# Forget gates as fp32 products in four column groups, bias copies split in eight, and weight splits ahead of row work

## The chip, the cores and the metric

The kernel runs on one core of one Trainium2 chip. Its time is the device time of one execution in microseconds (us); lower is better. The times given are the median of three runs with their lowest and highest; the profile is of one further execution.

## The reference, cut to what matters

One encoder layer is applied to two groups of tokens with shared weights: 528 prompt tokens (16 learned meta tokens and 512 frames) and 64 new frames of a running stream whose last 128 keys and values are cached. Everything is fp32.

```python
z = h @ w_in                       # 2048 -> heads' q, k, v, gates g, and 16 forget columns ff
lf = log_sigmoid(ff + b_f)         # one value per token and forgetting head
c = cumsum(lf)                     # over the tokens (prompt; cached 128 and then the 64 new)
# 16 forgetting heads ("Fox"):
s = q @ k.T * SCALE + c[query] - c[key];  s = where(key <= query, s, -1e30);  o = softmax(s) @ v
# 16 sliding-window heads in 4 key/value groups ("Swa"), T5 bias from rel_bias by distance, and a sink:
s = q @ k.T * SCALE + bias;  p = exp(s - m) / (sum(exp(s - m)) + exp(sink - m));  o = p @ v
mix = concat(o_fox * silu(g_fox), o_swa * silu(g_swa)) @ w_out
y = layer_norm(ALPHA * h + mix)
```

The outputs are y for both groups, the new keys and values of all heads, and `lf` itself.

## The kernel before, in words

**Tiling.** Activations lie transposed: 16 chunks (`ko`) of 128 features by 592 tokens (`TOK`), in two halves of 296 tokens (`HALF`). The projection weights come as 52 tiles of 128 output columns by 2048 features, those of the output as 16 more. To have nearly fp32 results from the fast fp32r product, each operand is split in a high part (a copy in fp32r, made by ScalarE, ACT) and a low part (raw minus high, made by VectorE, DVE), and a product is three matmuls: high by high, high by low, low by high. Two weight tiles make a "duo"; its halves of the features are combined as in Strassen's scheme, which gives 15 units of 12 matmuls for TensorE (PE) in a duo, and needs sums of weight blocks (`make_seven`, `make_five`, `make_six`, `make_four` on DVE), each of them split in high and low again (`seven_part`, `back_parts` and the like, on ACT and then on DVE).

**Stretches.** `whole` writes the same plan for each engine. A stretch is one or two duos; in it the projections of the next pair of heads stand on PE together with the attention of the pair before. The first stretch has one duo (`first=True`, 15 steps) and no attention; then come 8 stretches of two duos with Fox attention, 7 with Swa attention (one of two duos, six of one), and a final one that runs beside the output projection. Step `s` of a stretch holds unit `u` of its duo `k`. In each step every engine goes through a fixed list in order (`run` of each engine): what comes later in the list waits for all before it. Every engine works its queue in order.

**One tile of attention.** There are five query tiles to a pair. Tile i has its scores at step `score_at[i]` (PE `score`, DVE `scores`: bias, mask, maximum), exponentials a step later (ACT `probabilities`), reciprocals two steps later (DVE `reciprocals`, ACT `scale_rows`), transposes at `score_at[i] + 4` (PE `turn`), copied by ACT (`keep_turned`), and values (PE `values`).

**In a step of ACT before the change:** `keep_turned`, `probabilities`, `scale_rows`, then the weight parts of this step (`inside`), then the rest. **In a step of DVE:** `reciprocals`, the joins of a unit's result (`join`), `scores`, then `split(st, *ready)` (the low part of q or k, or the SiLU; each waits for ACT to evacuate first), `keep_values`, the low part of the cached keys, and only then the weight parts. The back half of the second tile of a duo (`back_parts(d, 1)`) is at u == 4 on ACT and at u == 6 on DVE; unit 8 is the first to need it.

**The opening.** `opening_products` on PE runs while x and the first two weight tiles (v, g) come in, in 9 parts of x (`X_CUTS`). Ahead of each part's products it makes the forget columns: weights `wff_parts` hold high, high again and low (48 columns), and each of them meets x high and x low in both halves: four matmuls of 296 columns to a chunk, into partitions 0 to 47 of `ps[:, O_BANK + h]`. The parts at 0, 16 and 32 are summed afterwards. The parts of `wff` are made by two ACT copies and a DVE subtraction before anything else.

**The gates before:** at step 1 (`LOGS_AT`) ACT copies partitions 32 to 47 of both banks to `e` (`gates`), DVE adds the bias and takes |z|, ACT takes exp(-|z|), DVE makes 1 + e, and a reciprocal of 16 rows by 592; ACT takes the logarithm. At step 4 (`SUMS_AT`) DVE finishes lf (written over the first rows of `kT`) and makes three running sums (`cT`). At step 1 and 2 stand also `last_sums`, the splits of the third sum of x blocks and of a changed x block, which unit 6 needs. `turn_gates` on PE at step 7 turns `cT`; `bias_table` on DVE at step 9 writes the rows of the Swa bias (31 small copies).

**GpSimd (POOL)** fills constants and issues DMAs, in order. Before the first stretch it waits for `bias_made` (the table), stores it, clears `q2`, waits for `c_ready`, stores `cT` and lf, clears `k_low`, `pt_meta`, `v_nat`; only then does it load the running sums (`cbc`), the cached keys (`kc`) and values. PE's unit at step 12 of the first stretch needs `zeros`, DVE's join of k needs `lf_stored`, since lf lies in `kT`. In the first Swa stretch POOL makes one DMA of all 16 rows of the bias to 128 copies each (`rel_copies`, DRAM to DRAM), waits for it, and loads the bias of each pair from it.

**SyncE (SP)** issues the weight loads, 512 KB each, each when the DVE's low part of the data before is made: `right_low`, `four_made`, `back_low[1]`, `back_low[0]`, in this order in each duo.

```python
                    for i in st.at(st.score_at, s - 2):      # ACT, ahead of the weight parts
                        scale_rows(st, i)
```

Of the kernel before, what the change touches and what calls it, by code (L numbers as in the profile page):

```python
# [24 lines left out]
F32 = mybir.dt.float32  # L25
# [5 lines left out]
P = 128  # L31
# [3 lines left out]
N_HEADS = 16  # L35
# [34 lines left out]
LOGS_AT, SUMS_AT, GATES_TURNED_AT, TABLE_AT, V_FIRST_AT = 1, 4, 7, 9, 12  # L70
LAST_SUMS_AT = 1
# [217 lines left out]
def build(nc, xT, w_all, w_ff, b_f, lf_cache, k_cache, v_cache, sinks, rel, keep_k, keep_v,  # L289
          x_p, x_s, ln_g, ln_b, y_p, y_s, fkT, fvT, lf_out, skT, svT, kept_k, kept_v):  # L290
    ctx = ExitStack()
    with ctx:
# [66 lines left out]
        bf = sb("bf", [N_HEADS, 1], F32)  # L359
# [6 lines left out]
        wff_parts = sb("wff_parts", [P, KO, 3, N_HEADS], F32R, at=cbc_at + TOK * 4)  # L366
# [4 lines left out]
        gate_terms = sb("gate_terms", [N_HEADS, 5, TOK], F32, at=keys_at)  # L371
        z, e, u1, wk, az = (gate_terms[:, i, :] for i in range(5))
# [42 lines left out]
        wff_high, wff_low = sem("wff_high"), sem("wff_low")  # L415
# [5 lines left out]
        x_high, x_low = sem("x_high"), sem("x_low")  # L421
        sum_made, sum_high, sum_low = sem("sum_made"), sem("sum_high"), sem("sum_low")
# [142 lines left out]
        def _(sp):  # L565
            sp.dma_start(wff, w_ff).then_inc(wff_loaded, 16)
            for what, i in opening:
# [5 lines left out]
                if what == "x" and i == 1:  # L573
                    for dst, src in ((bf[:], b_f), (lfc, lf_cache), (relT, rel),
                                     (sink[:], sinks.partition_broadcast(P))):
                        sp.dma_start(dst, src).then_inc(small_loaded, 16)
# [80 lines left out]
        def _(pool):  # L657
# [23 lines left out]
            pool.wait_ge(sum_made, 4)  # L681
            nc.gpsimd.memset(q2[:, 2 * NQ:].bitcast(F32), 0.0).then_inc(zeros, 1)
            pool.wait_ge(c_ready, 3)
            pool.dma_start(c_rows, cT[:]).then_inc(c_stored, 16)
            pool.dma_start(lf_out, lfT).then_inc(lf_stored, 16)
            pool.wait_ge(zeros, 2)
            nc.gpsimd.memset(k_low[HD:P, 0, :].bitcast(F32), 0.0).then_inc(zeros, 1)
            pool.wait_ge(zeros, 3)
            nc.gpsimd.memset(k_low[0:HD, 1, :].bitcast(F32), 0.0).then_inc(zeros, 1)
            pool.wait_ge(sum_low, 4)  # L690
            nc.gpsimd.memset(pt_meta[:], 0.0).then_inc(zeros, 1)
            pool.wait_ge(c_stored, 16)
            pool.wait_ge(cq_turned, 1)
            nc.gpsimd.memset(v_nat[:, Values.META, :], 0.0).then_inc(zeros, 1)
# [1335 lines left out]
```

## Time and profile before

| | |
|---|---|
| median of 3 runs | 1079.94 us (1077.12 to 1082.41) |
| the profiled execution | 1080.62 us, its span 1078.8 us |
| PE / DVE / ACT / POOL busy | 95% / 67% / 50% / 5% of the span |
| mean granted TensorE clock | 0.983 |
| DMA | 109 GB/s over the span |

The span is the time from the first to the last instruction. An engine's busy share counts the time in which at least one of its instructions ran. PE's idle time is what can be won or lost without changing its work; the granted clock says how fast it ran in a stretch.

### The profile page before, as it was taken

To read this page: it belongs to the slowest core of one execution; us is meant where nothing else is said; L and a number is where in the kernel's file an instruction comes from. 1 tells how busy PE (TensorE), PEld (TensorE's weight loads), DVE (VectorE), ACT (ScalarE), POOL (GpSimd) and SP (SyncE) were. 2 spreads that over 40 slices of the span, in tenths; PEclk is the share of its full clock that TensorE was granted. 3 is DMA by queue.
4 is the path that set the end of the run, shared out by engine and by line. 5 is a ranking of instruction groups with operands and counts; after the bars stand their busy time and mean duration, and the time that the engine had idled before them with its cause. 6 is when DMAs were issued, how large, how long until landed. Compare 5 with 4: busy or idle time off the path is not lost.

```text
span 1078.8 us, 20251 instructions
## 1 busy us (share of the span) xinstructions
PE 1025.7 (95%) x7287; PEld 951.8 (88%) x7287; DVE 721.0 (67%) x1454; ACT 534.2 (50%) x1219; POOL 58.8 (5%) x117
## 2 busy tenths in 40 slices
PE   8957999999999999999979999999999999999996
PEld 7957999999999999999979889899899878888884
DVE  6686768685867768685856877676776764332486
ACT  6425646464654646465544766564766672111310
POOL 1011000101000000100001000010000000000000
PEclk9978999999999999999989999999999999999998
DMA  9012322323232222323432322132322653222413
GB/s 334 32 64 89 106 92 77 128 89 116 86 110 72 92 99 89 132 89 99 154 113 76 109 88 72 52 104 69 109 89 94 240 194 101 79 78 94 179 60 117
DMA packets 31297, 115.00 MB, mean 107 GB/s; under 512 B 4352, under 2 KB 4768, under 8 KB 28624
## 3 DMA queue, kind: packets, MB, share of 16 engines
q1 hardware_dynamic: 24320, 87.26, 23.3%
q0 software_dynamic: 6928, 27.08, 7.4%
q8 instruction: 31, 0.51, 0.2%
q14 instruction: 18, 0.15, 0.0%
HBM read 99.31 MB, written 18.29 MB: 109 GB/s over the span
## 4 chain that ended last, share of the span: by engine, by line
PE 54%; DVE 20%; ACT 10%; issue 10%; DMA 4%; DVEq 1%; POOL 0%; SPq 0%; ACTq 0%; POOLq 0%
PE ps L1856 19%; PE ps L1618 16%; PE ps L1628 10%; DVE wl L1089 5%; PE ps L1822 4%; DMA w_raw<-in_w_all 3%; PE ps L1796 2%; ACT tb L901 2%; DVE tb L1266 2%; ACT k L879 1%; ACT q L874 1%; DVE small L1287 1%; DVE tb L1272 1%; ACT wh L815 1%; DVE small L1285 1%
## 5 line engine op out<-in xcount | busy, mean ns | idle before, releaser
L1618 PE MATMUL ps<-xh,wh 128*128 128x296 f32 (+1 forms) x864 | 264.2, 306 | 10.1 <-DVE wl L1089 9.7
L1618 PE MATMUL ps<-xh,wl 128*128 128x296 f32 (+1 forms) x864 | 257.6, 298 | 0.0
L1618 PE MATMUL ps<-xl,wh 128*128 128x296 f32 (+1 forms) x864 | 257.4, 298 | 0.0
L1856 PE MATMUL ps<-wh,mix_parts 128*128 128x512 f32 x576 | 186.2, 392 | 0.0
L1618 PEld LDWEIGHTS ps<-xh,wh 128*128 128x128 f32 x864 | 164.1, 190 | 17.2 <-DVE wl L1089 15.2
L1618 PEld LDWEIGHTS ps<-xl,wh 128*128 128x128 f32 x864 | 164.3, 190 | 0.0
L1618 PEld LDWEIGHTS ps<-xh,wl 128*128 128x128 f32 x864 | 163.9, 190 | 0.0
L1089 DVE TENSOR_TENSOR wl<-w_raw,wh 128x1024 fp32r<-128x1024 f32 (+1 forms) x150 | 142.9, 953 | 22.7 <-ACT wh L815 12.6
L1628 PE MATMUL ps<-xh,wh 128*128 128x296 f32 x400 | 123.4, 309 | 13.7 <-DVE mid_part L1164 7.3
L1856 PEld LDWEIGHTS ps<-wh,mix_parts 128*128 128x128 f32 x576 | 108.1, 188 | 24.2 <-issue 0.7
L901 ACT ACTIVATE tb<-tb,small 128x256 f32<-128x256 f32 (+5 forms) x160 | 81.3, 508 | 94.6 <-DVE small L1285 71.0
L1856 PE MATMUL ps<-wl,mix_parts 128*128 128x512 f32 x320 | 125.0, 391 | 0.0
L1628 PE MATMUL ps<-xl,wh 128*128 128x296 f32 x400 | 120.5, 301 | 0.0
L1628 PE MATMUL ps<-xh,wl 128*128 128x296 f32 x400 | 120.2, 301 | 0.0
L913 ACT ACTIVATE tb<-tb,small 128x256 f32<-128x256 f32 (+4 forms) x160 | 72.1, 498 | 40.8 <-DVE small L1300 40.1
L1628 PE MATMUL ps<-sum_high,wh 128*128 128x296 f32 x300 | 92.1, 307 | 0.0
L1628 PEld LDWEIGHTS ps<-xh,wh 128*128 128x128 f32 x400 | 76.4, 191 | 15.3 <-DVE xl L1089 7.5
L1628 PE MATMUL ps<-sum_low,wh 128*128 128x296 f32 x300 | 89.7, 299 | 0.0
L1628 PE MATMUL ps<-sum_high,wl 128*128 128x296 f32 x300 | 89.7, 299 | 0.0
L1085 DVE TENSOR_TENSOR wl<-w_raw,wh 128x1024 fp32r<-128x1024 f32 x32 | 38.1, 1222 | 69.0 <-ACT wh L803 68.9
L1628 PEld LDWEIGHTS ps<-xl,wh 128*128 128x128 f32 x400 | 76.6, 192 | 0.0
L1628 PEld LDWEIGHTS ps<-xh,wl 128*128 128x128 f32 x400 | 76.3, 191 | 0.0
(195 smaller groups left out, 1740.5 us busy)
## 6 DMA issues: line engine op xcount, KB each, us to landing
w_raw<-in_w_all SPq DMA_DIRECT2D x106, 512.0 KB, 3.9
w_raw<-in_w_all SPq DMA_DIRECT2D x14, 1024.0 KB, 4.8
cbc<-c_rows POOLq DMA_DIRECT2D x16, 360.0 KB, 4.2
x_raw<-in_xT SPq DMA_DIRECT2D x7, 592.0 KB, 10.1
rows<-in_x_p POOLq DMA_DIRECT2D x4, 1024.0 KB, 5.2
out_y_p<-rows SPq DMA_DIRECT2D x16, 256.0 KB, 2.5
mix_rows<-mixT POOLq DMA_DIRECT2D x14, 288.0 KB, 2.4
rel_copies<-rel_rows POOLq DMA_DIRECT2D x1, 3072.0 KB, 18.6
```

The source lines that it names most:

```text
L815: nc.scalar.activation(wh[f][:, BACK], w_raw[f][:, BACK], ACT.Copy).then_inc(back_high[f], 1)
L874: nc.scalar.activation(q2[r, at:at + width], home(f, h)[r, result(tile, h)], ACT.Copy, scale=SCALE).then_inc(q_high, 1)
L901: nc.scalar.activation(t, t, ACT.Exp, bias=nm, accum_out=total[:, i % 3, head:head + 1]).then_inc(exp_done, 1)
L913: nc.scalar.activation(row, row, ACT.Copy, scale=recip[:, i % 3, head:head + 1]).then_inc(scaled, 1)
L1085: nc.vector.tensor_tensor(wl[slot][:, a], w_raw[slot % 2][:, a], wh[slot][:, a].bitcast(F32), ALU.subtract).then_inc(w_low, 1)
L1089: nc.vector.tensor_tensor(low, raw, high.bitcast(F32), ALU.subtract).then_inc(done, 1)
L1266: ins = nc.vector.scalar_tensor_tensor(out=rows_[:, head, a:b], in0=st.score_out(ps, head, piece, b - a), scalar=cqp[:, i, head:head + 1], ...
L1618: ins = nc.tensor.matmul(ps[:, bank, result(tile, h)], a[f][:, w], b[:, ko, first:first + width], start=(ko == n_first and i == 0), stop=( ...
L1628: ins = nc.tensor.matmul(ps[:, bank, 0:HALF], a[:, w], b[:, j, :], start=(start and j == 0 and i == 0), stop=(stop and j == CUT - 1 and i ...
L1796: ins = nc.tensor.transpose(st.turn_out(ps, head, j), tb[:, i % SLOTS, head, first:first + P], ident[:])
L1822: ins = nc.tensor.matmul(ps[head_rows(head), bank, at:at + q], v_nat[:, block_, HD * head:HD * head + HD], moving[:, head, 0:q], start=(j ...
L1856: ins = nc.tensor.matmul(ps[:, bank, :], a, b[slot][:, w], start=(ko == 0 and i == 0), stop=(ko == KO - 1 and i == len(products) - 1))
```

## The change

In the opening, the forget columns are now plain fp32 products straight from `x_raw` and `wff`, without splits: for each chunk and half one product of 16 columns, even and odd chunks apart, each of the four in its own group of 32 columns of the array (`tile_position`), so that results lie at partitions 0, 32, 64 and 96. They wait for the DMA of x alone and stand ahead of PE's wait for `x_low`. The gate arithmetic works on one tensor of 80 partitions by 296 (half 0 at partition 0, half 1 at 64), and its steps are spread: inputs and 1 + e in `opening_splits`, reciprocals at step 3, logarithm and lf at step 5, running sums at step 7; `turn_gates` moves from step 7 to 9, `bias_table` from 9 to 13, v's turn from 12 to 13. `last_sums` goes into `opening_splits`. lf lies in `tb` and no longer in `kT`.

POOL's opening is in another order: cached keys first, then v's store, cT, the clears, the running sums, cached values, and the bias table and k's store last. The copies of the bias are made two heads at a time, one DMA at the start of each stretch that has Fox attention; the first Swa stretch waits for all eight.

In all stretches: ACT's `scale_rows` stands behind the weight parts of its step; DVE's `split`, `keep_values` and the low part of the cached keys too; `back_parts(d, 1)` moves to u == 3 on ACT and u == 5 on DVE.

```diff
-LOGS_AT, SUMS_AT, GATES_TURNED_AT, TABLE_AT, V_FIRST_AT = 1, 4, 7, 9, 12
-LAST_SUMS_AT = 1
+GATES_TURNED_AT, TABLE_AT, V_FIRST_AT = 9, 13, 13
+GATE_ROWS = 80
+BIAS_COPIES = FOX_PAIRS
...
-        gate_terms = sb("gate_terms", [N_HEADS, 5, TOK], F32, at=keys_at)
+        gate_terms = sb("gate_terms", [P, 5, HALF], F32, at=keys_at)
...
-        lfT = kT[0:16, :]
+        lfT = tb[0:16, 0, :, :].rearrange("p a b -> p (a b)")[:, 0:TOK]
...
# POOL
-            pool.wait_ge(bias_made, 1)
-            pool.dma_start(rel_rows, bias_rows).then_inc(bias_stored, 16)
-            ...
+            def first_loads(st):
+                pool.wait_ge(gates_summed, 1)
+                pool.wait_ge(x_low, X_PARTS)
+                nc.gpsimd.memset(gate_terms[0:GATE_ROWS, 0:2, :], 0.0).then_inc(z_cleared, 1)
+                pool.wait_ge(sum_made, 4)
+                nc.gpsimd.memset(q2[:, 2 * NQ:].bitcast(F32), 0.0).then_inc(zeros, 1)
+                pool.wait_ge(sum_low, 4)
+                nc.gpsimd.memset(pt_meta[:], 0.0).then_inc(zeros, 1)
+                pool.dma_start(kc[:], k_cache[0]).then_inc(k_cached, 16)
+                pool.wait_ge(v_read, 1)
+                pool.wait_ge(v_first, 1)
+                pool.dma_start(fvT[0:P, :], vT[:]).then_inc(v_stored, 16)
+                pool.wait_ge(c_ready, 3)
+                pool.dma_start(c_rows, cT[:]).then_inc(c_stored, 16)
...              # k_low cleared, lf stored, running sums loaded, v_nat cleared, cached values loaded
+                pool.wait_ge(bias_made, 1)
+                pool.dma_start(rel_rows, bias_rows).then_inc(bias_stored, 16)
...
+            def copy_bias(i):
+                two = bass.ds(2 * i, 2)
+                pool.dma_start(rel_copies[two], rel_rows[two, :].rearrange("h (o n) -> h o n", o=1)
+                               .broadcast_to([2, P, REL])).then_inc(bias_copied, 16)
...
-                if st.own is Swa and st.kind is Fox:
-                    pool.dma_start(rel_copies, ...16 heads...).then_inc(bias_copied, 16)
-                    pool.wait_ge(bias_copied, 16)
+                if st.kind is Fox:
+                    copy_bias(st.g)
...
# ACT, opening_splits
-                act.wait_ge(wff_loaded, 16)
-                nc.scalar.activation(wff_parts[:, :, 0, :], wff, ACT.Copy).then_inc(wff_high, 1)
-                nc.scalar.activation(wff_parts[:, :, 1, :], wff, ACT.Copy).then_inc(wff_high, 1)
...
                 front_parts(1, (passed, 1))
+                act.wait_ge(sum_made, 3)
+                nc.scalar.activation(sum3_high[:], raw3[:], ACT.Copy).then_inc(sum_high, 1)
+                act.wait_ge(z_cleared, 1)
+                act.wait_ge(gates_summed, 1)
+                for h in range(2):
+                    ins = nc.scalar.activation(gate_half(e, h), ps[HD * h + 32:HD * h + 32 + N_HEADS, O_BANK + h, 0:HALF],
+                                               ACT.Copy)
+                ins.then_inc(gates_joined, 1)
                 seven_part(1, (passed, 2))
                 six_part(1, (passed, 2))
+                act.wait_ge(sum_made, 4)
+                nc.scalar.activation(xh[:, first_x, late], x_raw[:, first_x, late], ACT.Copy).then_inc(sum_high, 1)
                 ...            # v's evacuation
                 back_parts(1, 0, (projected[1], 1))
+                act.wait_ge(gate_step, 2)
+                nc.scalar.activation(e, az, ACT.Exp, scale=-1.0).then_inc(gate_exp, 1)
                 ...            # the two Tanh
                 act.wait_ge(gate_step, 3)
                 nc.scalar.activation(az, u1, ACT.Ln).then_inc(gate_exp, 1)
...
# ACT, each step
-                    for i in st.at(st.score_at, s - 2):
-                        scale_rows(st, i)
...
-                        if u == 4:
+                        if u == 3:
                             back_parts(d, 1, (projected[1], 2) if st.first else (unit_done, st.after(k, -1)))
...
+                    for i in st.at(st.score_at, s - 2):
+                        scale_rows(st, i)
                     if st.kv is not None and s == st.cached_at:
                         cached_high(st)
...
# DVE, opening_splits
                 nc.vector.tensor_tensor(x21, x21, x22, ALU.subtract).then_inc(sum_made, 1)
+                gate_inputs()
+                dve.wait_ge(sum_high, 3)
+                low_of(sum3_low[:], raw3[:], sum3_high[:], sum_low)
+                gate_ones()
                 back_parts(1, 0)
-                dve.wait_ge(sum_made, 4)
                 for h in range(2):
                     silu(st, h, (first_part, diff_part)[h], ps[:, 2 + h, :])
+                dve.wait_ge(sum_made, 4)
+                dve.wait_ge(sum_high, 4)
+                low_of(xl[:, first_x, late], x_raw[:, first_x, late], xh[:, first_x, late], sum_low)
...
# DVE, each step
-                    if ready is not None:
-                        split(st, *ready)
-                    ...         # keep_values, low part of the cached keys
                     if inside:
...
+                        if u == 5:
+                            back_parts(d, 1)
                         if u == 6:
                             four_part(d)
-                            back_parts(d, 1)
...
+                    if ready is not None:
+                        split(st, *ready)
+                    ...         # keep_values, low part of the cached keys
                     if st.first:
-                        if s == LOGS_AT:
-                            ...
+                        if s == 3:
+                            gate_reciprocals()
+                        if s == 5:
                             gate_logs()
-                        if s == SUMS_AT:
+                        if s == 7:
                             gate_sums()
...
# PE, opening_products
+                def gate_products(two):
+                    for h in range(2):
+                        for odd in range(2):
+                            ko, to = 2 * two + odd, HD * h + 32 * odd
+                            ins = nc.tensor.matmul(ps[to:to + N_HEADS, O_BANK + h, 0:HALF], wff[:, ko, :],
+                                                   x_raw[:, ko, h * HALF:(h + 1) * HALF],
+                                                   start=(two == 0), stop=(two == KO // 2 - 1), tile_position=(0, to))
+                    return ins
...
-                    pe.wait_ge(x_low, i + 1 if i < X_PARTS - 3 else X_PARTS)
-                    for ko in ahead(i):
-                        ...
+                    for two in ahead(i):
+                        if two == ahead(i)[0] or i == X_PARTS - 3:
+                            pe.wait_ge(x_loaded[...the part that holds chunk 2 * two + 1...], 16)
+                        ins = gate_products(two)
                     if i == X_PARTS - 3:
                         ins.then_inc(gates_summed, 1)
+                    pe.wait_ge(x_low, i + 1 if i < X_PARTS - 3 else X_PARTS)
```

Waits that go with the moved data: DVE's join of the first k no longer waits for `lf_stored`, its first split of k waits for `zeros` 5 (was 4), its first score waits for `lf_stored`; ACT's first `keep_turned` waits for `bias_stored`; PE's first turn of v waits for `cq_ready` 2 as well.

## Rows read from the trace of the kernel before

**Rows 1.** The page, its part 1: busy time, share, instructions.
```profile
PE 1025.7 (95%) x7287; PEld 951.8 (88%) x7287; DVE 721.0 (67%) x1454; ACT 534.2 (50%) x1219; POOL 58.8 (5%) x117
```

**Rows 2.** Waits of PE, whole span: who waited for whom, us in total, times, longest.
```profile
PE ps L1618 <- DVE wl L1089: 9.7, 11, 3.2
PE ps L1628 <- DVE mid_part L1164: 7.3, 1, 7.3
PE ps L1628 <- DVE mid_part L1197: 6.4, 1, 6.4
PE ps L1822 <- ACT pt_meta L923: 4.9, 1, 4.9
PE ps L1796 <- ACT pt_meta L923: 4.5, 6, 0.9
...
PE ps L1796 <- ACT pt L921: 2.4, 5, 0.5
```

**Rows 3.** Windows: length; busy us of PE, PEld, DVE, ACT, POOL; PEclk; DMA share, GB/s.
```profile
59.60:66.30 6.70, 3.64 (x15) 3.67 (x16) 6.60 (x9) 0.63 (x1) 0.00 (x0) 0.50 0.27 97
...
69.90:76.50 6.60, 4.83 (x19) 4.83 (x20) 6.46 (x29) 0.46 (x1) 0.00 (x0) 0.50 0.23 79
...
90.30:97.00 6.70, 3.17 (x13) 3.17 (x14) 5.45 (x12) 2.58 (x4) 0.00 (x0) 0.50 0.01 2
...
547.80:554.40 6.60, 3.71 (x27) 3.32 (x28) 4.62 (x8) 4.25 (x9) 0.00 (x0) 0.50 0.04 14
```

**Rows 4.** Timeline of DVE, 38 to 82: start us, duration us, what, [idle before].
```profile
38.48 1.38 DVE L1374 TENSOR_TENSOR x_raw<-x_raw 128x1184 f32<-128x1184 f32 x1
...
51.33 0.95 DVE L1394 SCALAR_TENSOR_TENSOR gate_terms<-ps,bf,gate_terms 16x296 f32<-16x296 f32 x2 [4.66 <-ACT gate_terms L973]
...
54.82 3.84 DVE L1406 RECIPROCAL gate_terms<-gate_terms 16x592 f32<-16x592 f32 x1
...
66.07 1.25 DVE L1428 TENSOR_TENSOR_SCAN cT<-cbc,kT 16x528 f32<-16x528 f32 x1
...
75.14 2.27 DVE L1333 COPY pt<-pt 16x165 f32<-16x165 f32 x31
81.04 0.47 DVE L1197 TENSOR_TENSOR kT<-ps,diff_part 128x296 f32<-128x296 f32 x1 [3.63 <-DMA out_lf_out<-kT]
```

**Rows 5.** Timeline of ACT, 88 to 90.
```profile
88.36 1.26 ACT L892 ACTIVATE k<-kc 64x128 fp32r<-64x128 f32 x4 [4.94 <-DMA kc<-in_k_cache]
```

**Rows 6.** Timeline of PE: first matmul of unit 3, second duo.
```profile
101.28 0.30 PE L1628 MATMUL ps<-xh,wh 128*128 128x296 f32 x1
```

**Rows 7.** Timeline of PE: fp32 and fp32r products.
```profile
6.92 0.30 PE L1726 MATMUL ps<-xl,wff_parts 128*48 128x296 f32 x1
...
115.19 0.29 PE L1618 MATMUL ps<-xh,wl 128*128 128x280 f32 x1
115.42 1.09 PE L1822 MATMUL ps<-pt,v_nat 128*64 128x128 f32 x16
116.34 0.39 PE L1822 MATMUL ps<-pt_meta,v_nat 128*64 128x128 f32 x4
```

**Rows 8.** Timeline of ACT, DVE and PE in a Fox stretch, steps 4 to 8.
```profile
229.15 1.04 ACT L815 ACTIVATE wh<-w_raw 128x1024 fp32r<-128x1024 f32 x1
...
233.29 1.22 DVE L1089 TENSOR_TENSOR wl<-w_raw,wh 128x1024 fp32r<-128x1024 f32 x1
...
234.56 0.40 PE L1618 MATMUL ps<-xh,wh 128*128 128x280 f32 x1 [0.68 <-DVE wl L1089]
```

**Rows 9.** Timeline of DVE and ACT in a Swa stretch, steps 6 and 7.
```profile
642.27 0.45 DVE L1205 SCALAR_TENSOR_TENSOR mixT<-last_part,first_part 128x280 f32 x1 [1.69 <-ACT last_part L867]
...
644.77 0.91 ACT L913 ACTIVATE tb<-tb,small 128x256 f32<-128x256 f32 x2 [2.81 <-DVE small L1300]
```

**Rows 10.** The page's part 6, and ACT's timeline at 548.
```profile
rel_copies<-rel_rows POOLq DMA_DIRECT2D x1, 3072.0 KB, 18.6
...
548.52 1.06 ACT L809 ACTIVATE wh<-w_raw 128x1024 fp32r<-128x1024 f32 x1 [7.04 <-DMA w_raw<-in_w_all]
```

More of the change, by code:

```diff
@@ L715, in run @@
             def run(st):
+                if st.first:
+                    first_loads(st)
+                    return
                 g, kv = st.pair, st.kv
-                before = st.kind is not None
-                if st.own is Swa and st.kind is Fox:
-                    pool.dma_start(rel_copies, rel_rows.rearrange("h (o n) -> h o n", o=1)
-                                   .broadcast_to([N_HEADS, P, REL])).then_inc(bias_copied, 16)
-                    pool.wait_ge(bias_copied, 16)
+                if st.kind is Fox:
+                    copy_bias(st.g)
                 if st.turn_before is not None and not st.final:
@@ L737, in run @@
                 if st.own is Fox:
-                    pool.wait_ge(c_stored, 16)
-                    if before:
-                        pool.wait_ge(score_read, Fox.base(g))
+                    pool.wait_ge(score_read, Fox.base(g))
                     pool.sem_inc(pool_passed, 1)
@@ L766, in run @@
                                    ).then_inc(v_cached, 16)
-                    if before and not st.keep:
+                    if not st.keep:
                         store_mixed(st.g)
@@ L1189, in join @@
                 if h == 0 and tile == "k":
-                    if st.first:
-                        dve.wait_ge(lf_stored, 16)
-                    else:
+                    if not st.first:
                         dve.wait_ge(k_stored, 16 * st.kv)
@@ L1494, in run @@
                             five_part(d)
-                        if st.first and s == LAST_SUMS_AT + 1:
-                            last_sums()
                         if u == 4:
@@ L1698, in ahead @@
                 def ahead(i):
-                    if i > X_PARTS - 3:
+                    if i == 0 or i > X_PARTS - 3:
                         return ()
-                    return range(x_part(i).start, KO if i == X_PARTS - 3 else x_part(i).stop)
+                    return range(x_part(i).start // 2, KO // 2 if i == X_PARTS - 3 else x_part(i).stop // 2)
+                def gate_products(two):
+                    for h in range(2):
+                        for odd in range(2):
[4 more added lines that the diff above has]
+                    return ins
                 def some(k, h, chunks):
@@ L1832, in turn_values @@
                     pe.wait_ge(zeros, 7)
+                    pe.wait_ge(cq_ready, 2)
                 else:
```

134 lines of the change are left out of this document (55 added, 79 removed).

## The prediction

> **What bounds the kernel now.** The page's first part comes first: PE is busy for 95% of the span [rows 1], all others far less, so its work is the floor, and what is to be won lies in its idle time and its clock. Next the waits of PE over the whole span [rows 2]. Three groups are seen. In the first duo stand 7.3 us (before unit 6), 3.2 (before unit 8; the longest of the first row) and, before unit 0 of the second, 6.4. A single wait of 4.9 us stands before values at 550 us. The rest are small ones that come back in nearly each stretch: 6.5 us of L1618 on the back half of the second weight tile (9.7 minus 3.2), and 4.5 plus 2.4 us of transposes on ACT. Then the granted clock [rows 3]: after each long wait PE runs at 0.50, that is 1.2 GHz where 2.4 is the upper level. Of these windows PE works 3.64, 4.83, 3.17 and 3.71 us, and half of each is lost to the clock: 7.7 us in all, 5.8 of it in the first duo.
>
> DVE's timeline tells what the first duo waits for [rows 4]. From 51.33 DVE makes the gates in one piece, a reciprocal of 3.84 us among them, and the results that PE waits for stand behind. Later its join of k waits until lf has gone out by DMA (81.04), a DMA that POOL issues only after the table (75.14 and 2.27). ACT then waits 4.94 us for cached keys whose load stands behind the same POOL queue [rows 5]. So the first duo is bound by gates, table and POOL's order, not by PE.
>
> **The change, part by part.** The sums go against the profiled execution: 1080.62 us, span 1078.8, so 1.8 us lie around the span; the median of the runs shown is 0.7 lower.
>
> *Gates on PE.* Removed are 64 fp32r products of 296 columns (one of them in [rows 7]), one column per pulse of 2.4 GHz, 0.135 us from start to start with a little overhead. Added are 32 fp32 products of 296 columns. For their price: the values of one tile are ten fp32 products of 128 columns in two column groups and stand as 16 plus 4 records, two to a product; they take from 115.42 to 116.5 until the last one starts, about 0.107 us for each product, so 0.21 us for two side by side. At 296 columns one product is then 0.49 us. If four groups run side by side, 8 fours take 4.0 us; if only two do, 7.9; if none, 15.8. I take 4.0, since the row with groups shows full overlap, for two. Of it 0.5 us falls into times when PE waits for x anyway, while 60 of the old products (8.1 us) stood where PE is busy: a gain of about 4.5 us; 1.2 with two side by side, minus 5.7 with none.
>
> The Trainium skill ("TensorEngine Tiling (Array Packing)", Key Properties) says that a change of tiling mode drains the engine. The trace agrees in kind: 0.23 us pass from the last product before the block to its first, against 0.135 elsewhere [rows 7]. By that rule six insertions would cost about 1.2 us more, which lies in the bounds above.
>
> *The chain of DVE and ACT in the opening.* It decides, not the gates on PE, so I walk it with durations of rows. DVE's changed block of x ends at 38.48 + 1.38 = 39.86, as before (all ahead of it waits for DMA or is unchanged). Then inputs 0.95 and |z| 0.49 (half the columns), low part of the third sum 1.38, two small steps 0.55, back part 1.22 [rows 8], two SiLU 0.92, with some 0.9 of waiting for ACT's exp: 46.4. ACT may keep the first result 0.45 later, so unit 3 starts at about 46.9. ACT's block of x delays v's evacuation to 41.7, where PE, 4.5 us earlier, waits at most 0.5.
>
> DVE goes on: low part of the block 1.38, difference 0.46, five 0.68, middle 0.46, reciprocal 1.95 (half of 3.84): 51.1. Two weight parts 1.36, back part 1.22, four steps of logs 1.9: 55.6. Join, four, q's low parts, the two sums of five: 2.7. Running sums 1.25 and about 0.65: 60.2. PE, now without waits, has done unit 9 at 58.3 and waits 1.9 us to turn the gates. Then front, two sums, join, six: 3.7; k's low parts wait for ACT: 65.1; the cached keys, on whose load nobody waits now, 67.0; gates kept 67.35. PE comes to turn v at 65.5 and waits 1.8 us for that. At step 13 the table of 2.27 us and v's copies lie on DVE, so the last join of the duo ends at 75.75, where PE wanted its bank at 74.6: 1.2 us. The key's low parts and scores follow, and unit 3 of the second duo begins at 78.7. Before it began at 101.28 [rows 6]. The gain is 22.6 us; clock and waits that the rows of before show there are all in it. It is a walk of some forty steps without gaps, so I take 21, with ends of 12 and 26: 12 where two of the new waits let the clock fall and the chain slips by some 7 us, 26 where PE meets none of the new waits. The lower price of PE's gates changes this by little: 3 us more on PE are taken out of the two waits behind.
>
> *The bias copies.* Removed is the DMA of 3072 KB that took 18.6 us [rows 10]; the weight loads issued into it came so late that ACT waited 7.04 us, and PE 4.9. Eight copies of 384 KB at the start of stretches are 2.3 us each by that row. They lie beside a moment at which the loads under way are for a back half needed far later, so I cost them at nothing; without that cover each could hold ACT by up to 2.3 us, of which PE would see perhaps half, 9 us in all. Gain: 4.9 plus 1.9 of clock = 6.8, ends minus 2 and 6.8. POOL issues one DMA more per stretch, 0.5 us, ahead of v's store; whoever waits for that store has many steps.
>
> *Second tile's back half.* DVE ends it at 234.51 and PE's unit 8 starts at 234.56 after a wait of 0.68 [rows 8]. It stands at step 6 behind a join, scores of 2.6 us and another part. At step 5 it would end about 3.5 us earlier, since ACT has its high part made at step 3, in idle time, and no longer at 229.15. Gain 6.5 us [rows 2]; the end below is 0. What is late next: the scores of step 6 start 1.2 us later, and the exponentials and the transposes behind them; they have two steps (3.3 us) in hand.
>
> *Row scales and splits behind the weight parts.* In the Swa stretch DVE stands 1.69 us for a tanh and ACT 2.81 us for a reciprocal [rows 9], with weight parts queued behind both. These parts now fill such waits; the reciprocal comes 1.5 us earlier, ACT's copies too, by about 2 us. PE's waits there are 0.5 to 0.9 us [rows 2], so they go: 6.9 us, ends minus 5 and 6.9. What is queued behind the moved instructions: ACT's copies of the transposes, up to 1.9 us later where no wait is filled (step 13), for which PE has a step in hand. I take 6.0.
>
> *Sum.* 21 + 6.8 + 6.5 + 6.0 = 40.3. 1080.6 - 40.3 = 1040.3 for the execution, 0.7 lower for the median: I say 1040.
>
> **The rivals.**
>
> A: *the first duo gives half.* The gate chain is now on the path at steps 9 and 13. If POOL's longer chain (three clears, two loads of running sums, then v's places) or the cached keys hold PE for another 3 us at two places, and the clock falls after each, 10 us of the gain are gone: 1050. For it speaks that POOL's issues took 0.5 us each and that three such waits cut the clock before [rows 3]; against it, that POOL's part ends by 64.9 in my walk. 10%.
>
> B: *the repeated waits only move.* In every stretch the transposes wait for ACT, which now has the scales behind parts that themselves wait for PE's units. Then 12.5 us are not won: 1053. For: the scores at step 6 are later. Against: both engines have idle times of over 1 us in rows 9. 10%.
>
> C: *it is slower.* Place: ACT at steps 2, 5 and 11, where a part waits for a unit's end and the scales now wait behind it. PE's transposes need them two steps later. If that margin is gone, PE, ACT and DVE run in a lock step, and each such tile costs PE two parts of 0.6 us: 3.5 tiles of a stretch by 1.2 by 15 stretches are 63 us, 1103. It decides from 2.7 us lost per stretch on. Against it: the unit that the parts wait for is done a step before. 4%.
>
> D: *four column groups don't overlap.* The Trainium skill ("TensorE: Matmul & The Clock Gate", What overlaps and what doesn't) has matmuls start strictly in order; by that, two records on one group would let only neighbours overlap. As a mechanism of this kernel: at 15.8 us for the 32 products PE's opening ends some 10 us later than in my walk, of which 3.7 are taken out of the waits behind: 1047. With two side by side it stays at 1041. 6%.
>
> **How the numbers follow.** My forecast has 70%, 1034 to 1048 by itself; A, B and D 26% together, 1047 to 1053; C 4%. The range that leaves out about 2 in 10 goes from 1032 to 1055: the low end where the first duo gives 26 and all else its upper end, the high end past B. Faster by over 0.5% (5.4 us, about what a measurement of this kernel can tell from no change): all but C, and a rest for what I haven't seen: 0.93. Within: 0.02. Slower: 0.05.
>
> **What would show it.** Unit 3 of the second duo near 79 us, no wait of PE over 3 us before it, and waits on the turn of gates and of v of 1 to 3 us. The fp32 gate products in fours, four starting together every 0.25 us. No wait at 540 to 550, rel_copies eight times at 3 to 5 us. No wait of L1618 on DVE of 0.68 in the Fox stretches, and none of L1796 in the Swa ones. It is wrong if PE's waits after 110 us sum to over 10 us, or if its busy time rises by more than 5 us.

## The result and the profile after

| | before | after |
|---|---|---|
| median of four runs | 1080.25 us (1077.12 to 1082.41) | 1030.16 us (1030.02 to 1030.48) |
| span of the profiled execution | 1078.8 us | 1028.6 us |
| mean granted TensorE clock | 0.983 | 0.997 |

The kernel became faster by 4.6%: the ratio is 0.9539, with a 95% interval of 0.9515 to 0.9563. The median lies 9.8 us under the forecast of 1040 and 1.8 us under the low end of the range. The sign and the places of the gain were right, and its size was not: 50.2 us of span where the sum had 40.3. One execution of experiment 8's kernel took 3469.64 us, for which no row gives a reason; it is left out below.

The page of the kernel after, its parts 1, 2 and 4 (they answer to [rows 1]; the chain's PE share was 54% before):

```profile
PE 1006.8 (98%) x7287; PEld 936.7 (91%) x7287; DVE 718.2 (70%) x1454; ACT 532.7 (52%) x1217; POOL 66.7 (6%) x125
...
PEclk9999999999999999999999999999999999999998
...
PE 90%; DVE 4%; DMA 2%; issue 1%; ACT 1%; SPq 1%; DVEq 0%; ACTq 0%
```

Waits of PE, whole span, after; columns as in [rows 2]:

```profile
PE ps L1627 <- DVE wl L1357: 1.8, 1, 1.8
PE ps L1734 <- DVE vT L1344: 1.6, 1, 1.6
PE ps L1859 <- DVE cq L1446: 1.6, 1, 1.6
PE ps L1627 <- DVE xl L1349: 1.5, 1, 1.5
PE ps L1839 <- ACT pt_meta L941: 1.2, 2, 0.9
PE ps L1765 <- DVE cT L1438: 1.2, 1, 1.2
PE ps L1637 <- ACT vT L977: 1.1, 1, 1.1
PE ps L1637 <- DVE kT L1200: 0.8, 1, 0.8
...
```

Read them against [rows 2]. The repeated rows (10 of the 11 waits of L1618, 6 and 5 of L1796) are gone, and so are the three of over 3 us and the one at 550. Eight kinds are left, seven of them single ones in the first duo; the longest is 1.8 us, and after none does the clock fall. The windows that answer to [rows 3], with the same columns, are 20 to 60 us, the end of the first duo, and the stretch around 514.39, where the product starts that waited at 550 before:

```profile
20.00:60.00 40.00, 37.72 (x296) 34.72 (x294) 37.82 (x48) 21.77 (x30) 2.24 (x6) 1.00 0.38 144
60.00:78.00 18.00, 15.59 (x116) 15.12 (x115) 14.72 (x59) 9.13 (x20) 6.35 (x12) 1.00 0.30 84
509.50:521.50 12.00, 12.00 (x104) 11.66 (x103) 9.51 (x21) 8.65 (x20) 0.00 (x0) 1.00 0.16 59
```

DVE's timeline after, in the first duo (it answers to [rows 4]): the reciprocal, a running sum, cached keys, gates kept, the table, the join.

```profile
48.78 1.99 DVE L1411 RECIPROCAL gate_terms<-gate_terms 80x296 f32<-80x296 f32 x1
...
57.68 1.24 DVE L1438 TENSOR_TENSOR_SCAN cT<-cbc,tb 16x528 f32<-16x528 f32 x1
...
65.73 0.59 DVE L1236 TENSOR_TENSOR k_low<-kc,k 64x128 fp32r<-64x128 f32 x2 [1.69 <-ACT k L908]
...
66.49 0.15 DVE L1446 COPY cq<-ps 64x16 f32<-64x16 f32 x1
...
71.09 2.27 DVE L1338 COPY pt<-pt 16x165 f32<-16x165 f32 x31
...
74.43 0.45 DVE L1200 TENSOR_TENSOR kT<-ps,last_part 128x296 f32<-128x296 f32 x1
```

ACT's and PE's timelines after: the cached keys, which waited 4.94 us in [rows 5]; unit 3 of the second duo, at 101.28 in [rows 6]; a block of four gate products between two others.

```profile
64.43 1.27 ACT L908 ACTIVATE k<-kc 64x128 fp32r<-64x128 f32 x4
...
77.67 0.30 PE L1637 MATMUL ps<-xh,wh 128*128 128x296 f32 x1
```

```profile
9.04 0.29 PE L1627 MATMUL ps<-xh,wl 128*128 128x296 f32 x1
9.26 0.69 PE L1718 MATMUL ps<-x_raw,pt 128*16 128x296 f32 x8
9.89 0.41 PE L1627 MATMUL ps<-xh,wh 128*128 128x296 f32 x1
```

The block is four fp32 products (two records each) and takes 9.89 - 9.26 = 0.63 us with the change back to whole-array products.

The Fox stretch of [rows 8] and the Swa stretch of [rows 9], after:

```profile
197.45 1.04 ACT L831 ACTIVATE wh<-w_raw 128x1024 fp32r<-128x1024 f32 x1
...
203.83 1.22 DVE L1094 TENSOR_TENSOR wl<-w_raw,wh 128x1024 fp32r<-128x1024 f32 x1
...
208.45 0.30 PE L1637 MATMUL ps<-sum_high,wl 128*128 128x296 f32 x1
208.59 0.29 PE L1627 MATMUL ps<-xh,wh 128*128 128x280 f32 x1
...
601.11 0.45 DVE L1208 SCALAR_TENSOR_TENSOR mixT<-last_part,first_part 128x280 f32 x1 [0.19 <-issue]
...
602.55 0.89 ACT L929 ACTIVATE tb<-tb,small 128x256 f32<-128x256 f32 x2
```

DVE now ends its low part at 205.05, 3.5 us ahead of unit 8; it ended 0.05 us ahead before. DVE's wait of 1.69 is 0.19, and ACT's of 2.81 is gone.

The bias copies (page, part 6, answering to [rows 10]), and the one place where a copy is seen to hurt:

```profile
rel_copies<-rel_rows POOLq DMA_DIRECT2D x8, 384.0 KB, 10.7
...
391.77 1.06 ACT L825 ACTIVATE wh<-w_raw 128x1024 fp32r<-128x1024 f32 x1 [1.73 <-DMA w_raw<-in_w_all]
...
393.94 0.77 PE L1839 MATMUL ps<-pt,v_nat 128*64 128x128 f32 x10 [0.94 <-ACT pt_meta L941]
```

**Where the 50.2 us came from.** From unit 3 of the second duo on, PE issues the same 6786 matmuls in the same order in both kernels, so they can be laid side by side, start against start. Up to that unit 101.28 - 77.67 = 23.6 us are gained, behind it 26.5 more. Of these the stall at 550, with the slow clock behind it, is 6.8. The other 19.7 are the repeated waits, net of 1.0 given back at 393.94 and 0.6 in the first Fox stretch. The idle time shown on the 21 waits that went was 6.5 plus 6.9, so 13.4 us (13.5 unrounded).

Why more comes back than is shown can be read in three rows of PE's timeline before, around the wait of [rows 8] (its own row, 234.56, stands there):

```profile
233.45 0.29 PE L1628 MATMUL ps<-sum_low,wh 128*128 128x296 f32 x1
233.58 0.30 PE L1628 MATMUL ps<-sum_high,wl 128*128 128x296 f32 x1
...
234.79 0.29 PE L1618 MATMUL ps<-xl,wh 128*128 128x280 f32 x1
```

One product starts 0.13 us after the other (233.45, 233.58), yet each record is 0.30 long: it ends 0.16 us past the time at which the next would have started. Idle time is counted from that end. The wait shows 0.68, but from start to start 0.98 us pass where after the change 0.14 do (208.45 to 208.59): 0.84. The second product then starts 0.23 after the first instead of 0.13. So 0.95 us were lost where 0.68 are shown. In the alignment eight of the ten repeated waits of L1618 cost this 0.27 us more than they show, ten of the eleven of L1796 0.21 more, and three waits 0.07 more or nothing: 17.8 us for the 21, 4.3 more than shown. At eleven more places (nine of L1618, two of L1796) a product started 0.23 to 0.34 us late, with 0.07 us or less shown as idle: 3.2 us. 13.5 + 4.3 + 3.2 - 1.0 - 0.6 = 19.4; the last 0.3 is spread over small steps.

The Trainium skill ("Perfetto Trace Analysis", Tensor Engine Instruction) says that TensorE's end times are estimated, not observed. The rows agree: ends lie 0.16 us past the next start.

### The profile page after: what moved, and what is told of

Read it like the earlier page. It is cut to its first block, busy times and chain, and to the rows that moved or that the text cites. A ratio compares the mean times of both kernels' runs of the same rounds, so it can differ in the third digit from the quotient of the medians.

```text
span 1028.6 us, 20283 instructions
## 1 busy us (share of the span) xinstructions
PE 1006.8 (98%) x7287; PEld 936.7 (91%) x7287; DVE 718.2 (70%) x1454; ACT 532.7 (52%) x1217; POOL 66.7 (6%) x125
## 3 DMA queue, kind: packets, MB, share of 16 engines
q0 software_dynamic: 11856, 27.14, 8.0%
## 4 chain that ended last, share of the span: by engine, by line
PE 90%; DVE 4%; DMA 2%; issue 1%; ACT 1%; SPq 1%; DVEq 0%; ACTq 0%
PE ps L1627 30%; PE ps L1637 27%; PE ps L1874 20%; PE ps L1839 5%; PE ps L1813 4%; PE ps L1797 2%; PE ps L1796 2%; DMA x_raw<-in_xT 1%; DMA w_raw<-in_w_all 1%; DVE wl L1094 1%; PE ps L1859 1%; SPq L572 0%; PE ps L1817 0%; DVE tb L1271 0%; SPq L575 0%
## 5 line engine op out<-in xcount | busy, mean ns | idle before, releaser
L1627 PE MATMUL ps<-xh,wh 128*128 128x296 f32 (+1 forms) x864 | 261.3, 302 | 3.2 <-DVE wl L1357 1.8
L1627 PEld LDWEIGHTS ps<-xh,wh 128*128 128x128 f32 x864 | 162.5, 188 | 9.2 <-issue 6.2
L1627 PEld LDWEIGHTS ps<-xl,wh 128*128 128x128 f32 x864 | 162.8, 188 | 0.0
L1627 PEld LDWEIGHTS ps<-xh,wl 128*128 128x128 f32 x864 | 162.2, 188 | 0.0
L1637 PEld LDWEIGHTS ps<-xh,wh 128*128 128x128 f32 x400 | 75.2, 188 | 2.5 <-ACT vT L977 1.3
L1637 PEld LDWEIGHTS ps<-xl,wh 128*128 128x128 f32 x400 | 75.5, 189 | 0.0
L1637 PEld LDWEIGHTS ps<-xh,wl 128*128 128x128 f32 x400 | 75.1, 188 | 0.0
## 6 DMA issues: line engine op xcount, KB each, us to landing
rel_copies<-rel_rows POOLq DMA_DIRECT2D x8, 384.0 KB, 10.7
```

Of the source, the lines that this page charges most:

```text
L1627: ins = nc.tensor.matmul(ps[:, bank, result(tile, h)], a[f][:, w], b[:, ko, first:first + width], start=(ko == n_first and i == 0), stop=( ...
L1637: ins = nc.tensor.matmul(ps[:, bank, 0:HALF], a[:, w], b[:, j, :], start=(start and j == 0 and i == 0), stop=(stop and j == CUT - 1 and i ...
```

## Experiments

Four kernels start from the one before and make one part of the change alone, or three of its four; the others start from the kernel after. Each ratio is against runs of the kernel before taken beside that experiment (medians 1079.0 to 1079.8 us). Gains "from 101.28 on" are from the alignment described above, one trace each: ahead of that unit the traces with the old opening differ among themselves (it starts at 99.5 to 102.4 us).

**1. The back half of the second tile alone.**

```diff
-                        if u == 4:      # ACT; on DVE 6 becomes 5
+                        if u == 3:
                             back_parts(d, 1, ...)
```

> The kernel before with one edit: the back half of the second tile is split at u == 3 (ACT) and u == 5 (DVE). Theory S (a wait of PE costs what passes from start to start, which is about 0.16 us more than the idle time shown, because a matmul's record ends 0.16 us past the next one's start, and the second matmul after a wait starts 0.1 us late as well): all waits of L1618 on DVE go, and with them the small ones of 0.07 us that the table of waits leaves out: 11 us less, ratio 0.990. Theory I (a wait costs the idle time shown): 6.5 us less, ratio 0.994. If a new wait takes their place: under 3 us.

1065.85 us (1063.22 to 1066.94), ratio 0.9869 [0.9849, 0.9888]. From 101.28 on, 14.3 us are gained, against a sum of 6.5: 15.5 in the repeated waits, less 1.2 at the stall of 550, which got longer. Of PE's repeated waits these are left; all of L1618 are gone:

```profile
PE ps L1797 <- ACT pt L921: 2.4, 5, 0.5
PE ps L1797 <- ACT pt_meta L923: 1.7, 2, 0.9
```

A Fox stretch gives 1.28 us (0.95 + 0.33), which the start-to-start cost explains; the Fox stretches give 9.5 us in all, the Swa stretches 6.0. Of these 6.0, 2.0 are waits of L1618, and 3.8 are waits of L1796 (four of the eleven went), which the prediction had put down to the row work alone.

**2. The row work behind the weight parts alone.**

```diff
# ACT: scale_rows(st, i) from ahead of inside(...) to behind it
# DVE: split, keep_values and the cached keys' low part from ahead of the weight parts to behind them
```

> The kernel before with one edit: scale_rows on ACT and the splits, keep_values and the low part of the cached keys on DVE stand behind the weight parts of their step. Theory S: the waits of the transposes in the Swa stretches go (4.5 + 2.4 us shown, eleven of them): 8.7 us less, ratio 0.992. Theory I: 6.9 us less. The rival that the moved work makes transposes late elsewhere: less than 3 us, and new waits of L1796 in the Fox stretches. In the first duo, where the gates are still in one piece, either way within 1 us.

1059.12 us (1057.12 to 1060.85), ratio 0.9814 [0.9794, 0.9835]. From 101.28 on, 20.9 us: 3.4 at the stall of 550 (it shows 3.3 now), 17.5 in the repeated waits, against a sum of 6.0. The waits of L1796 are gone. Those of L1618 are shorter, about 0.25 us each (the longest of this row, 1.1, is in the first duo):

```profile
PE ps L1618 <- DVE wl L1089: 3.1, 9, 1.1
```

In the alignment that is 5.4 us in the Fox stretches and 12.1 in the Swa ones. Both theories had this far too low, since both gave each edit only one kind of wait. The measurement says that the two edits overlap: the back half alone takes all of what is lost in the Fox stretches and half of it in the Swa ones, the row work alone all in the Swa stretches and more than half (5.4 of 9.5) in the Fox ones.

**3. The bias copies alone.**

```diff
-                if st.own is Swa and st.kind is Fox:
-                    pool.dma_start(rel_copies, ...16 heads...)
+                if st.kind is Fox:
+                    copy_bias(st.g)
```

POOL's wait for the copies moves to the first stretch that loads a bias.

> The kernel before with one edit: eight bias copies of two heads at the start of the Fox stretches in place of one. The wait of 4.9 us of PE at 550 and the fallen clock behind it go: both theories 6.9 us less, ratio 0.9936. Should the copies delay weight loads, as one seems to in the changed kernel (ACT waits for a load at 390), 1 us of it is given back once or more.

1074.81 us (1073.71 to 1076.11), ratio 0.9953 [0.9937, 0.997]. 5.6 us from 101.28 on: the 6.8 of the stall, less 1.1 where ACT waits 3.18 us for a weight load beside a copy (issued at 409.24), and PE for ACT at 425.03:

```profile
PE ps L1826 <- ACT pt_meta L927: 1.1, 1, 1.1
```

In this trace unit 3 of the second duo started 1.1 us later than before, at 102.38, so the spans differ by 4.6 only. Being 0.5% of the time, this part is as small as such a comparison can tell.

**4. All three together, without the opening.**

> The kernel before with all three edits, so that only the opening and the gates are as before. Theory S: 26.5 us less, ratio 0.9755, and its first duo like that of the kernel before (unit 3 of the second duo near 101). Theory I: 19 to 20 us less, ratio 0.982; the rest of what the whole change gained would then have come from the first duo.

1051.36 us (1049.79 to 1053.89), ratio 0.974 [0.9718, 0.9761]. 27.6 us from 101.28 on, where the three alone add up to 40.8. They aren't additive: without the stall of 550 it is 20.9 us in the repeated waits, against 15.5 + 17.5 for experiments 1 and 2, which in part take the same waits away. The first duo still has its long waits:

```profile
PE ps L1633 <- DVE mid_part L1168: 7.3, 1, 7.3
PE ps L1846 <- POOL v_nat L695: 5.3, 1, 5.3
PE ps L1633 <- DVE mid_part L1201: 4.3, 1, 4.3
```

Its span is 1050.4, that of the kernel after 1028.6: gates and opening are worth 21.8 us (22.9 before unit 3 of the second duo, 1.1 given back behind it).

**5. Seven of eight gate products left out** (only the last block of four is made, so that the forget columns are of two chunks of the input alone).

> The changed kernel with only the last four of the 32 fp32 gate products (the forget columns are then of two chunks of the input alone; all else is the same). PE's opening is 7 blocks of 0.63 to 0.9 us shorter. Theory C (the chain of DVE and ACT sets the end of the first duo): v's evacuation and the gates' steps come no earlier, unit 3 of the second duo stays at 77.7 within 0.5, total 1030 within 0.7. Theory P (PE's products are on the path): 4 us less, 1026.

1031.06 us (1030.22 to 1031.82), ratio 0.9553 [0.953, 0.9577]: nothing won. What PE saves comes back as one longer wait, 4.9 us where it was 1.1, and around its end 6.8 us at the lower clock (39.6 to 46.5, granted 0.50). Unit 3 of the second duo starts at 78.73, 1.1 us later than in the kernel after and outside the 0.5 that was expected: 0.5 of it is there when the long wait ends (42.47 against 42.01), the rest comes behind it, where the clock is low at first.

```profile
PE ps L1637 <- ACT vT L977: 4.9, 1, 4.9
```

**6. Four gate products in two column groups** (odd chunks in the columns of the even ones, in other banks, from which ACT then copies them; the results are the same).

```diff
-                            ko, to = 2 * two + odd, HD * h + 32 * odd
+                            ko, to, bank = 2 * two + odd, HD * h, ((O_BANK + h, (T_BANK, SIDE)[h])[odd])
```

> The changed kernel with the odd chunks' gate products in the same two column groups as the even ones, in other banks: at most two products side by side. If four groups do run side by side, a block of four products takes about 0.5 us more than the 0.63 of the changed kernel (1.0 to 1.2 from its first start to the next product). In total, theory C: 0 to 0.5 us more, since PE has 3.7 us of waits behind it; theory P: 4 us more.

1030.73 us (1030.11 to 1032.15), ratio 0.9553 [0.9528, 0.9577], not told apart from four groups. PE's timeline, the same block:

```profile
9.16 1.18 PE L1718 MATMUL ps<-x_raw,pt 128*16 128x296 f32 x8
10.28 0.40 PE L1627 MATMUL ps<-xh,wh 128*128 128x296 f32 x1
```

10.28 - 9.16 = 1.12 us against 0.63: a second pair adds 0.49, the price that the prediction had for one product. So four groups do work side by side, and 8 blocks save 3.9 us of PE, nearly all of it hidden. What the new gates bring is then DVE's, ACT's and POOL's: their work was cut, spread and put in another order, and PE's was not the bound. Which of the three brings how much of the 22.9 us no run here takes apart.

**7. The copy of the bias in one piece, but early** (one DMA of 3072 KB at the start of the second stretch).

> The changed kernel with one bias copy of 3072 KB at the start of the second stretch in place of eight of 384 KB. Theory L (a copy this long holds up any weight load issued into its 18 us): loads issued at 83 to 85 land late by 8 to 10 us, PE stands 4 to 6 us and its clock falls: 6 to 7 us more, 1037. Rival M (only the moment in the first Swa stretch was bad): no change, 1030.

1036.6 us (1036.16 to 1037.78), ratio 0.9603 [0.958, 0.9626]. It lies from 76.42 to 95.30 us; three weight loads issued at 83.35 to 85.86 land at 93.79 to 97.63. The wait, and a window behind it (length, busy us of the five engines, clock, DMA):

```profile
PE ps L1840 <- ACT pt_meta L942: 6.7, 1, 6.7
...
95.40:102.00 6.60, 3.42 (x25) 3.10 (x26) 4.33 (x7) 4.25 (x9) 0.00 (x0) 0.52 0.02 8
```

It costs 6.9 us behind unit 3 of the second duo, about what the stall at 550 cost. So the eight pieces help since each is short, not since they come early.

**8. The bias table in idle time of DVE** (after the second part of x), the gates turned at step 10 and kept at the head of step 11.

> The changed kernel with the bias table made on DVE in its idle time after the second part of x (9.3 to 11.6 us), the gates turned at step 10 and kept at the head of DVE's step 11. Theory C: three waits of PE go (gates 1.2, v's turn 1.6, the last join 0.8, each 0.16 more from start to start): 4.1 us less, 1026. Rival: POOL's clears and loads, which end at about 65, take the place of the second wait, and k's join of the third: 1 to 2 us less, 1028.5.

1028.85 us (1028.4 to 1029.77, three executions), ratio 0.9531 [0.9501, 0.956]: about 1 us, which the ratios don't tell from none. The waits on `cT` and `kT` went, but the one on `cq` grew:

```profile
PE ps L1860 <- DVE cq L1449: 2.8, 1, 2.8
```

The copy of the gates stood at the head of step 11, behind the cached keys' low part of step 10, which waits for ACT until 65.7. Its place in DVE's list was wrong (mended in 12).

**9. The back half late again, in the kernel after.**

> The changed kernel with one edit undone: the second tile's back half stands again one step later on ACT and DVE. Theory T (each of PE's repeated waits has two causes in DVE's and ACT's order, and either edit takes most of them away): in the kernels built on the one before, the step alone gave 14.3 us from 101.28 us on, the row work alone 20.9, the bias copies 5.6, and all three together 27.6; so without the step 27.6 - (20.9 + 3.5) = 3.2 us come back, about 1033.5, as small waits of L1627 in the Fox stretches. Rival S (the edits add up): 11 to 14 us come back, 1041 to 1044.

1034.15 us (1034.05 to 1034.44), ratio 0.9581 [0.9565, 0.9597]: 4.0 us come back, as small waits, all in the Fox stretches in the alignment. That is near the 3.2 of theory T, and far from the 11 to 14 of its rival. The row of PE's waits:

```profile
PE ps L1626 <- DVE wl L1094: 2.6, 8, 0.8
```

**10. The row work ahead again, in the kernel after.**

> The changed kernel with the other edit undone: scale_rows on ACT, and the splits, the kept values and the cached keys' low part on DVE, stand ahead of the weight parts again. Theory T: 27.6 - (14.3 + 5.6) = 7.7 us come back, about 1038, nearly all of it in the Swa stretches, as waits on pt (L1796); next to nothing in the Fox stretches. Rival S (the edits add up): 17 to 21 us, 1047 to 1051, in both kinds of stretches.

1040.56 us (1039.85 to 1041.05), ratio 0.9639 [0.9623, 0.9655]. 10.4 us come back; in the alignment 1.5 of them before unit 3 of the second duo, 2.5 in the Fox stretches and 6.0 in the Swa ones. Two rows of PE's waits and one of ACT's timeline:

```profile
PE ps L1839 <- ACT pt_meta L941: 3.2, 6, 1.5
PE ps L1813 <- ACT pt L939: 2.5, 5, 0.5
...
151.67 1.06 ACT L825 ACTIVATE wh<-w_raw 128x1024 fp32r<-128x1024 f32 x1 [0.73 <-DMA w_raw<-in_w_all]
```

The second row is in the Swa stretches, as expected. The first is in the Fox stretches, where the theory had expected next to nothing. The third shows ACT waiting for a weight load some 14 us after a bias copy was issued (137.83), and the same stands at 212.04 and 272.42; that ACT has less in hand for it with the row work ahead is argued, not shown. Experiments 9 and 10 bear out that the edits overlap: undone singly they give back 4.0 and 10.4, where alone they had gained 15.5 and 17.5 in the repeated waits. They also fit experiments 1 and 2 place by place: the 4.0 are what the row work alone had left in the Fox stretches (9.5 - 5.4), and the 6.0 are the half of the Swa waits that the back half alone had left.

**11. The bias copies with the 128 copies outermost.**

```diff
-                pool.dma_start(rel_copies[two], ....rearrange("h (o n) -> h o n", o=1).broadcast_to([2, P, REL]))
+                pool.dma_start(rel_copies[two].rearrange("h p n -> p h n"),
+                               ....rearrange("h (o n) -> o h n", o=1).broadcast_to([P, 2, REL]))
```

> The changed kernel with each of the eight bias copies walked in another order: the 128 copies are the outermost dimension and the two heads the inner one, same bytes. Theory E (the 10.7 us from issue to landing come from the outermost dimension of two, which leaves the 384 KB to few of the 16 DMA engines): landing falls to 3 to 4 us, the one copy that meets ACT's weights near 390 us no longer does, and the time is 0 to 1.5 us lower, 1029. Rival F (a cost of each copy whatever its shape, or of the DRAM it writes): it stays near 10.7 us, and so does the wait.

1029.47 us (1029.07 to 1030.64), ratio 0.954 [0.9524, 0.9556], not told apart in time. The page, parts 6 and 3, and the row of PE's waits in which the 0.94 of 393.94 stood:

```profile
rel_copies<-rel_rows POOLq DMA_DIRECT2D x8, 384.0 KB, 5.1
...
q0 software_dynamic: 7120, 27.08, 7.9%
...
PE ps L1840 <- ACT pt_meta L942: 0.2, 1, 0.2
```

That wait is gone; the 0.2 that the row still has is another, at the first values. Behind unit 3 of the second duo 1.4 us are gained in the alignment. Landing falls from 10.7 to 5.1 us, not quite to 3 to 4, and the queue's packets from 11856 to 7120 for the same bytes. The order of the dimensions is the cause of half of the time. The trace's packets show how: a copy's 84 data packets of 4608 bytes take 7.9 us with two heads outermost, and 2.0 of them are under way at a time on average; with the 128 copies outermost, 80 such packets take 2.9 us, 6.7 at a time (medians of the eight copies). Some 1.7 us pass before the first of them and 0.4 behind the last. The 588 packets of 12 bytes that each copy had, and that are gone, run for some 2 us beside the first data packets; these go on for 6 us more. The Trainium skill ("DMA: Bandwidth & Descriptors", Rules for kernel authors) says that an outermost dimension of c < 16 keeps a DMA on at most c engines. The trace agrees: two heads were outermost, and two packets were under way.

**12. All that the experiments point to:** the table in idle time, the gates turned and kept in step 10 ahead of the cached keys, and the copies of 11.

> The changed kernel with the waits left in its opening worked away: the bias table in DVE's idle time after the second part of x, the gates turned and kept at step 10 and kept ahead of the cached keys, and the bias copies with 128 outermost. Theory G: the waits of PE on cq 1.6, on cT 1.2 and on kT 0.8 us go, and the copy's 0.9, each worth 0.16 us more than it shows: about 4 to 5 us less than the changed kernel, 1026. Rival H: what stands next in the order (POOL's clears for cached values, ACT's copy of v) holds PE instead, and 2 us at most are won: 1028.

1026.06 us (1025.91 to 1026.17), ratio 0.9505 [0.9489, 0.9521]: the fastest of all, 4.1 us below the kernel after, whose runs lie apart from it (the intervals of the ratios still touch). Of PE's waits these are left of the rows spoken of:

```profile
PE ps L1639 <- ACT vT L978: 1.7, 1, 1.7
...
PE ps L1639 <- DVE kT L1201: 0.6, 1, 0.6
PE ps L1861 <- DVE cq L1450: 0.6, 1, 0.6
```

In the alignment 2.4 us are gained before unit 3 of the second duo and 1.7 behind it.

## Why the prediction was wrong in its size

**The step that failed** is the pricing of the repeated waits, in the parts "second tile's back half" (6.5) and "row scales and splits" (6.0). It took the idle time shown on each wait as what its removal brings. Measured were 19.7 us for the two, net of the 1.0 lost to a copy. Of the difference of 7.2, 4.3 are what the 21 waits cost from start to start beyond the idle time shown, 3.2 are late starts that no row of the waits shows, and 0.9 the discount on 6.9 that nothing supported; the copy takes 1.0 off and the first Fox stretch 0.6, and 0.4 are small change and rounding. The bound "6.9" was thus no upper bound, and the low end of the range was set with it.

**The same step put each edit to the wrong account.** It gave the waits of L1618 to the back half (6.5) and those of L1796 to the row work (6.0). Alone they gain 15.5 and 17.5 us, together 20.9: the back half also cures four of the eleven waits of L1796, and the row work most of those of L1618. For L1618 the order of the lists says why: the weight part that unit 8 needs stands behind row work, so it comes in time if it starts a step earlier, and comes sooner if the row work stands behind it. Why an earlier back half cures waits of the transposes is not shown. That each wait has two cures did no harm to the sum, by luck: both edits were made, and the whole of the waits was counted once.

**The first duo** was taken at 21 where the walk gave 22.6 and 23.6 were measured. The walk held step by step: reciprocal 1.95, measured 1.99; table 2.27; running sums done at 60.2, measured 59.6; gates kept at 67.35, measured 66.64; last join at 75.75, measured 74.88; unit 3 at 78.7, measured 77.67. PE's waits on the turn of the gates, on the turn of v and before the last join were taken at 1.9, 1.8 and 1.2 us and measured 1.2, 1.6 and 0.8; the one on v's evacuation, "at most 0.5", was 1.1. Two sums of the walk are off by 0.1, which changes nothing (its terms give 46.3 and 51.2 where it has 46.4 and 51.1). Rounding the gain down because the walk is "some forty steps" had no row behind it and cost 1.6 of the 2.6. Experiment 4 confirms the place: 21.8 us hang on the opening.

**Gates on PE:** right in mechanism and price (0.63 us a block with the change back, where 0.5 plus changes was taken), and right that it matters little: experiments 5 and 6 change PE's share by 4 us and the time by under 1.

**The bias copies:** the gain was right, 6.8 us, the pieces were not: "2.3 us each", expected to land in 3 to 5, land in 10.7. The price divided the time of one long copy by eight; but the long copy, with 16 heads outermost, had 10 data packets under way at a time, and each small one 2 (the traces of before and after). The cover named for them, loads under way for a back half needed far later, failed once, at 391 us, for 1.0 us; experiments 7 and 11 show why.

**The rivals:** A and B are refuted (no wait over 1.8 us, repeated waits gone), C too, and D by experiment 6. Of the signs named, the landing of the copies failed; the others came, the gate products in fours 0.26 us apart among them. 40.3 + 2.6 + 7.2 = 50.1 us, of 50.2.

## What to carry to other kernels

Price a removed stall by the difference of start times of the matmuls on both sides of it, not by the idle time shown: here 0.68 us shown were 0.95, and at eleven places 0.23 to 0.34 us were lost with next to nothing shown. Before two edits are given separate sums, ask whether each cures the same wait. A small DMA isn't cheap by its bytes: look at which dimension is outermost, and at the loads queued behind it.

## What the runs showed of the hardware that was not expected

- In a stream of fp32r matmuls of 296 columns the records end 0.16 us past the start of the next one, so short waits of PE are under-counted: starts 0.23 to 0.34 us late show as 0.07 us of idle time or as nothing.
- 384 KB from DRAM to DRAM took 10.7 us with two heads outermost, two data packets at a time, and 5.1 with the 128 copies outermost, 6.7 at a time; 3072 KB took 18.6 in one piece.
- Four fp32 products of 16 by 296 in four column groups take 0.63 us together, in two groups 1.12.
